# A hybrid decoder step on one core: the gate's conditioning in five visits of two to four units in place of eight of two, with three more places for its weights

## What is computed

```
mod = silu(c) @ ada_w + ada_b                 # c: 9 conditioning vectors, ada_w: 2048 x 6144
shift, scale, gate = split(mod, 3)
h = rmsnorm(x, g_pre) * (1 + scale) + shift
z = h @ w_in                                  # pooling and retention branches read z
ya = y_a @ w_a_proj                           # pooling branch, gated by silu
yb = y_b @ w_b_proj                           # retention branch, group-normed, gated
g_a, g_b = split(sigmoid(h @ w_merge + b_merge), 2)
out = rmsnorm((g_a * ya + g_b * yb) @ w_out, g_post)
y = x + gate * out                            # gate = the last third of mod
```

## Time and profile before

| what | value |
|---|---|
| median of 3 runs | 929.7 us |
| the profiled execution, its time | 929.46 us |
| the profiled execution, its span in the trace | 927.6 us |
| mean granted TensorE clock | 0.997 |
| TensorE matmul busy | 911.0 us, 98% of the span |
| TensorE weight load busy | 873.8 us, 94% |
| VectorE busy | 554.2 us, 60% |
| ScalarE busy | 420.3 us, 45% |
| GpSimd busy | 54.9 us, 6% |
| read from HBM, written | 219.33 MB, 14.38 MB |

### The profile page before, as it was taken

The page is one execution under the profiler, slowest core; times in us unless marked ns, Lnnn a source line. Parts: engine busy times, 40 slices in busy tenths (PEclk is TensorE's granted clock), DMA queues, the critical chain, the costliest instruction groups (busy, mean ns, idle before and its releaser), DMA issues.

```text
span 927.6 us, 18788 instructions
## 1 busy us (share of the span) xinstructions
PE 911.0 (98%) x7816; PEld 873.8 (94%) x7816; DVE 554.2 (60%) x809; ACT 420.3 (45%) x537; POOL 54.9 (6%) x38
## 2 busy tenths in 40 slices
PE   6999999999999999999999999999999999999997
PEld 4888889999999999999999999999999999999997
DVE  4667776467575766757576655336454434446664
ACT  3424237556465665646454433444343434343330
POOL 0000000001102020120202122000000000000000
PEclk9999999999999999999999999999999999999999
DMA  9999985848576584857675555466787676744535
GB/s 365 420 420 418 419 330 198 323 145 318 182 292 231 206 301 152 323 188 275 243 274 177 194 203 188 152 272 189 279 309 289 243 259 241 258 156 177 182 137 187
DMA packets 43467, 234.58 MB, mean 253 GB/s; under 512 B 8848, under 2 KB 14224, under 8 KB 16656
## 3 DMA queue, kind: packets, MB, share of 16 engines
q1 hardware_dynamic: 43408, 233.72, 68.2%
HBM read 219.33 MB, written 14.38 MB: 252 GB/s over the span
## 4 chain that ended last, share of the span: by engine, by line
PE 93%; DMA 4%; DVE 1%; SPq 1%; POOL 1%; issue 0%; ACT 0%; DVEq 0%; POOLq 0%
PE bank L442 25%; PE bank L443 25%; PE bank L444 25%; DMA raw<-first_w 4%; PE bank L507 3%; PE bank L508 3%; PE bank L509 3%; PE bank L416 2%; PE bank L426 2%; PE bank L657 1%; PE bank L702 1%; PE bank L641 1%; DVE raw L1564 1%; PE bank L552 1%; PE bank L642 0%; PE bank L666 0%
## 5 line engine op out<-in xcount | busy, mean ns | idle before, releaser
L442 PE MATMUL bank<-h_hi,w_hi 128*128 128x264 f32 x1280 | 368.2, 288 | 0.0
L443 PE MATMUL bank<-h_lo,w_hi 128*128 128x264 f32 x1280 | 362.8, 283 | 0.0
L444 PE MATMUL bank<-h_hi,w_lo 128*128 128x264 f32 x1280 | 362.5, 283 | 0.0
L1132 DVE TENSOR_TENSOR w_lo<-raw,w_hi 128x2048 fp32r<-128x2048 f32 x119 | 272.3, 2288 | 141.2 <-PE bank L444 139.4
L792 ACT ACTIVATE w_hi<-raw 128x2048 fp32r<-128x2048 f32 x120 | 229.8, 1915 | 40.9 <-DMA raw<-stream 20.9
L442 PEld LDWEIGHTS bank<-h_hi,w_hi 128*128 128x128 f32 x1280 | 241.1, 188 | 6.1 <-issue 5.8
L443 PEld LDWEIGHTS bank<-h_lo,w_hi 128*128 128x128 f32 x1280 | 241.3, 189 | 0.3
L444 PEld LDWEIGHTS bank<-h_hi,w_lo 128*128 128x128 f32 x1280 | 240.1, 188 | 0.0
L442 PE MATMUL bank<-yb_hi,w_hi 128*128 128x264 f32 x256 | 72.8, 284 | 0.0
L507 PE MATMUL bank<-h_hi,w_hi 128*128 128x264 f32 x240 | 71.7, 299 | 1.1 <-DVE gate_sum L1165 0.9
L442 PE MATMUL bank<-m_hi,w_hi 128*128 128x264 f32 x256 | 72.7, 284 | 0.0
(11 more groups left out here) (189 smaller groups left out, 1205.9 us busy)
## 6 DMA issues: line engine op xcount, KB each, us to landing
raw<-stream SPq DMA_DIRECT2D x120, 1024.0 KB, 5.0
ada_ring<-ada SPq DMA_DIRECT2D x31, 1024.0 KB, 19.4
raw<-first_w SPq DMA_DIRECT2D x16, 1024.0 KB, 16.0
gate_ring<-ada SPq DMA_DIRECT2D x16, 1024.0 KB, 6.9
s_t<-sret SPq DMA_DIRECT2D x8, 1024.0 KB, 5.0
v_all<-v_dram SPq DMA_DIRECT2D x8, 1024.0 KB, 6.7
nret_s<-s_t SPq DMA_DIRECT2D x8, 1024.0 KB, 7.8
x_t<-xT SPq DMA_DIRECT2D x4, 528.0 KB, 6.0
```

What stands on the lines that cost most here:

```text
L442: pe.matmul(out, wh[:, cols], hi[:, k, :], start=(k == 0), stop=False)
L443: pe.matmul(out, wh[:, cols], lo[:, k, :], start=False, stop=False)
L444: mm = pe.matmul(out, wl[:, cols], hi[:, k, :], start=False, stop=(k == depth - 1))
L1132: dve.tensor_tensor(lo, raw[:, c % 3, :], hi.bitcast(f32), ALU.subtract).then_inc(lo_ready, 1)
```

## The change

The visits become five, after q = 3 (units 0 to 3), 7 (4 to 7), 18 (8 to 10), 23 (11 to 13) and 28 (14 and 15). Three more places hold conditioning weights: `cond_lo` over the second half of `m_lo`, `cond_hi` over the second half of `m_hi`, and `cond_ya` over the first tiles of `ya_out`, each at a time when what lies there is not needed. `COND_PLACE` gives each unit's place, `COND_LOADS` the turn q of SyncE's loop in which it is issued (its main load and its gates come first in the turn). Unit 0 is issued ahead of the loop.

```diff
-COND_VISITS = (3, 7, 11, 14, 18, 22, 26, 29)
+COND_VISITS = {3: (0, 1, 2, 3), 7: (4, 5, 6, 7), 18: (8, 9, 10), 23: (11, 12, 13), 28: (14, 15)}
+COND_PLACE = (0, 1, 2, 3, 0, 1, 2, 3, 0, 1, 4, 0, 1, 4, 0, 1)
+COND_LOADS = {0: 1, 1: 2, 3: 3, 4: 4, 5: 5, 6: 6, 7: 7, 11: 8, 12: 9, 13: 10, 19: 11, 20: 12, 21: 13, 24: 14, 25: 15}
...
+        with ExitStack() as far:
+            sb("under_hi", [128, KT // 2, NT], f32, far)
+            cond_hi = sb("cond_hi", [128, UNIT], f32, far)
         m_hi = sb("m_hi", [128, KT, NT], f32r, late)
+        with ExitStack() as near:
+            cond_ya = sb("cond_ya", [128, UNIT], f32, near)
         ya_out = sb("ya_out", [128, KT, NT], f32, late)
+        with ExitStack() as far:
+            sb("under_lo", [128, KT // 2, NT], f32, far)
+            cond_lo = sb("cond_lo", [128, UNIT], f32, far)
...
-        gate_loaded = [sem(f"gate_loaded{s}") for s in range(2)]
+        gate_loaded = [sem(f"gate_loaded{s}") for s in range(5)]
...
+        COND = [gate_ring[:, 0, :], gate_ring[:, 1, :], cond_lo[:, :], cond_hi[:, :], cond_ya[:, :]]
...
-            def load_cond(v, s):
-                if v >= 1:
-                    sp.wait_ge(gate_used, 2 * v - 1 + s)
-                sp.dma_start(gate_ring[:, s, :], ada1[2 * v + s]).then_inc(gate_loaded[s], 16)
+            def load_cond(u):
+                place = COND_PLACE[u]
+                if u == 3:
+                    sp.wait_ge(proj_done, 80)
+                elif u == 10:
+                    sp.wait_ge(mf_ready, FIRST // 2)
+                elif place in COND_PLACE[:u]:
+                    last = max(n for n in range(u) if COND_PLACE[n] == place)
+                    sp.wait_ge(gate_used, last + 1)
+                sp.dma_start(COND[place], ada1[u]).then_inc(gate_loaded[place], 16)
...
-            load_cond(0, 0)
-            load_cond(0, 1)
+            load_cond(0)
...
-                for s in range(2):
-                    if q - 1 - s in COND_VISITS[:7]:
-                        load_cond(COND_VISITS.index(q - 1 - s) + 1, s)
+                if q in COND_LOADS:
+                    load_cond(COND_LOADS[q])
...
                 if q in COND_VISITS:
-                    v = COND_VISITS.index(q)
-                    if v == 4:
-                        pe.wait_ge(gpart_ready, 1)
-                    for s in range(2):
-                        pe.wait_ge(gate_loaded[s], 16 * v + 16)
-                        gate_unit(2 * (v % 4) + s, gate_ring[:, s, :]).then_inc(gate_used, 1)
+                    for u in COND_VISITS[q]:
+                        if u == 8:
+                            pe.wait_ge(gpart_ready, 1)
+                        pe.wait_ge(gate_loaded[COND_PLACE[u]], 16 * COND_PLACE[:u].count(COND_PLACE[u]) + 16)
+                        gate_unit(u % 8, COND[COND_PLACE[u]]).then_inc(gate_used, 1)
```

## The result

| | before | changed |
|---|---|---|
| median | 929.6 us (5 runs, 929.2 to 929.8) | 950.1 us (5 runs, 947.6 to 951.3) |
| span of the profiled execution | 927.6 us | 948.7 us |
| mean granted clock | 0.997 | 0.987 |
| TensorE matmul busy | 911.0 us | 916.9 us |

The ratio is 1.0216, with a 95% interval of 1.0205 to 1.0228: the changed kernel is slower by 20.5 us, and 20.0 us was forecast (949.5 us).

A forecast was written before the change was run, and what follows sets the result against it. TensorE, busy throughout the merge stage, was taken as the bound, so added waits cost full length. Unit 3's 8.6, units 6 and 7's 9.0, clock 3.4, less 1.0 saved, gave 20.0 us: 949.5 us, range 938 to 956.

The forecast's parts named there:

- The view that decided: SyncE's queue timeline beside landing times: TensorE cannot start a unit before it lands, after its issue in program order.
- The wait for unit 3: Visit after projection 3: unit 3, issued behind column 4's gates, makes TensorE wait 8.6 us (ends 4.9 and 9.9).
- The shifted pattern: A later load pattern in the old trace, shifted 25.32 us: column 4's gates leave at 649.10, unit 3 at 649.94.
- Units 6 and 7: Visit after projection 7: TensorE waits 4.9 us for unit 6, 4.1 us for unit 7, 9.0 us together.
- The clock: TensorE at half speed behind both new waits: 1.7 us lost for each, 3.4 us together; ends 0 and 6.8.
- The visits: TensorE: three visits fewer, each with a fixed 0.33 us price for leaving the projection and returning, save 1.0 us.
- The later visits: Visits after projections 18, 23 and 28: loads land in time, cost 0; about 1 us a visit otherwise.
- only unit 3 would be waited for: Rival: TensorE waits only for unit 3, or the second wait is near its lower end; 940.4 us, chance 0.16.
- the main units starve: Rival: late main units hold TensorE some 3 to 6 us at projections 8 to 11; 953 to 956 us, chance 0.12.
- there is no wait: Rival: unit 3 lands before 647.07, so only the saving remains; 928.7 us, chance 0.02.

The follow-up runs named there:

- the exchange of the two steps: Changed kernel with each SyncE turn's conditioning unit issued ahead of the two gates, not behind them; 939.8 us, ratio 1.0109.
- the throwaway work: Changed kernel with throwaway 128-column matmuls into a free bank ahead of the waits for units 3, 6 and 7; 945.7 us, ratio 1.0161.

## Why the prediction was right

- **The view that decided.** That units 3, 6 and 7 stand in SyncE's order behind gates that wait for a projection shortly ahead of their own visit: for unit 3 the one just ahead, for units 6 and 7 the one before that. Shown by the changed kernel's queue, for units 3 and 6 by the exchange of the two steps, for unit 7 by the version with all loads early.
- **The wait for unit 3**, forecast 8.6 us, measured 8.66. The shifted pattern had the evacuation of projection 3 at 647.14, the gates at 649.10 and the issue at 649.94; measured were 647.22, 649.18 and 650.02, and the landing took the 5.8 us between 650.02 and 655.86 where 5.7 was taken. Reading only the unchanged times, 4.9 us, would have missed nearly half of it: the loads that the change moves delay the very gates that the late unit stands behind.
- **Units 6 and 7**, forecast 9.0 us, measured 7.1. This term was sized too high. Two things account for most of it. The issue that held SyncE for 1.30 us did not come this time (0.43 us), so both units landed some 0.9 us sooner in the visit. And unit 6 ran at half speed, so that 0.8 us of what was counted as waiting for unit 7 was spent in unit 6.
- **The clock**, forecast 3.4 us, measured 6.3 (2.8 and 3.5). This term was too low by nearly half in the profiled execution; in the second trace of the same kernel it was 4.8 us (1.5 and 3.3). The step that failed took the length of the slow stretch from the single one at the start of the kernel. Here the slow stretch behind the long wait lasted 5.8 us after the restart, not 3.3. The length of the wait alone does not explain it: the start-up's unit behind 3.41 us still ran at full speed, and in the second trace of the changed kernel the one behind 3.42 us ran at half. The upper end of the term, 6.8 us, did cover it. That the idle is the cause is shown by the throwaway work; what sets the size of the loss stays open.
- These two errors, -1.9 and +2.9 us, nearly cancel. Of each, 0.8 us is the same time, that of unit 6, which the forecast had as wait and the account here as slow clock; the rest, -1.1 and +2.1 us, cancels in part by luck. The sum of 20.0 us against 21.1 us of span is closer than its terms deserve.
- **The visits**, forecast -1.0 us. Shown at both sides: 1.2 us less for three visits fewer (0.6 to 2.2), 2.4 us more for eight visits more (1.3 to 3.0).
- **The later visits** cost nothing but their price, as forecast: in the changed kernel there is no wait behind 695.
- **The rivals.** That only unit 3 would be waited for: no, and with unit 3 early the second visit keeps its waits. That the main units starve: TensorE never waits for `w_lo` in the changed kernel, and with two conditioning loads in one turn it is busy throughout. That there is no wait: it takes another order of issues, and the version that has it gains 1.2 us.

## What to carry to other kernels

Before work is put together into fewer, larger steps, follow each operand back to its issue and to what the issuing queue waits for just ahead of it: here a load stood behind a transfer that depends on the projection right before the reader, and the idle time that the queue had earlier was of no use to it. Price a regrouping by its fixed cost per switch (0.33 us here) and ask what a single late operand would cost beside it (8.66 us and 2.8 us of low clock). And when a change moves loads, carry the delays that they cause through the chain before reading off the late one; the same pattern may stand elsewhere in the trace, and shifting it hit the issue of unit 3 to 0.1 us. What a transfer or an issue takes that once is not sure to come again: the 1.30 us did not.

## What the runs showed of the hardware beyond what was expected

- The clock that a wait leaves behind differs from one wait to the next, even at equal length. After a wait of 8.66 us TensorE ran at 0.50 for 5.8 us; after one of 8.61 us in the same program it lost only half as much. After waits of 3.90 us and of 3.42 us the next unit took 1.94 us, so the clock was low at once; behind 3.79 us it fell within the unit (1.69 us); behind 4.27 us the unit still took 1.07 us, full speed, and the clock fell after it (0.68 from 680 to 685). After waits of 2.49, 1.79 and 1.74 us the next unit took 1.07 us.
- SyncE's issue of a column's second gate, 132 KB, takes 0.43 us nearly always. Once or twice in most traces it takes longer, at changing columns: 1.30 us before, 0.95 us with unit 3 early, 1.08 us with all loads early, 1.58 and 1.87 us with the throwaway work, 0.79 us with sixteen visits, 1.00 us with the steps exchanged, and never in the two traces of the changed kernel. What stands right behind it is issued later by as much. The cause stays open.
